# Chunked gated delta rule inside a two-layer block: token-major output of a chunk pair, its per-token norm on ScalarE, and a rewritten order of the mixer

## What is computed

```
proj = rms_norm(x) @ w_in            # attention q, k, v; delta q, k, v; gate z; beta, decay
attn = dilated_attention(q, k, v)    # 8 heads of 64
q = q * rsqrt(sum(q*q) + EPS) * K**-0.5;  k = k * rsqrt(sum(k*k) + EPS)     # 4 delta heads of 128
T = inverse(I + strict_lower(k_beta k^T * decay))       # per chunk of 64 tokens
scan over 8 chunks:
    v_new = u_i - w_i @ state
    o     = q_i @ state + (q_i k_i^T * decay) @ v_new
    state = state * gl + k_i^T @ v_new
dn_out = rms_norm(o, dn_norm_w) * silu(z)               # norm over the 128 values of a head, per token
x = x + rms_norm(concat(attn, dn_out) @ w_out)          # then a gated FFN
```

## Time and profile before

| | us |
|---|---|
| median of 3 runs | 3020.96 (3014.07 to 3027.36) |
| profiled execution | 3016.94 |
| its span in the trace | 3015.1 |
| PE busy | 2863.4 (95%) |
| DVE, ACT, POOL busy | 1192.5, 1126.0, 1225.2 (37 to 41%) |
| mean granted clock of PE, of full speed | 0.96 |

### The profile page before, as it was taken

The page is one execution under the profiler, slowest core; times in us unless marked ns, Lnnn a source line. Parts: engine busy times, 40 slices in busy tenths (PEclk is TensorE's granted clock), DMA queues, the critical chain, the costliest instruction groups (busy, mean ns, idle before and its releaser), DMA issues.

```text
span 3015.1 us, 44190 instructions
## 1 busy us (share of the span) xinstructions
PE 2863.4 (95%) x15452; PEld 2294.6 (76%) x15452; DVE 1192.5 (40%) x2248; ACT 1126.0 (37%) x1894; POOL 1225.2 (41%) x630
## 2 busy tenths in 40 slices
PE   9998999999999979999999988999999998899997
PEld 7777777888887767778888666778778666778776
DVE  3554426553065542455512576410013566410012
ACT  3453234443244622444433324532333324532331
POOL 2323033555433221355544452255553452255553
PEclk7998989999999989999999999999999998999998
DMA  3211012223322100122232211122222111122222
GB/s 117 73 47 43 2 49 71 96 95 100 104 68 74 44 29 13 52 84 96 92 105 91 66 63 50 36 83 98 91 98 84 59 65 48 37 83 98 91 97 91
DMA packets 62876, 217.29 MB, mean 72 GB/s; under 512 B 6576, under 2 KB 6704, under 8 KB 62480
## 3 DMA queue, kind: packets, MB, share of 16 engines
q1 hardware_dynamic: 62416, 214.28, 21.6%
q0 software_dynamic: 320, 1.12, 0.2%
HBM read 213.28 MB, written 2.10 MB: 71 GB/s over the span
## 4 chain that ended last, share of the span: by engine, by line
PE 79%; DVE 7%; ACT 4%; POOL 4%; issue 3%; DVEq 1%; ACTq 0%; DMA 0%; POOLq 0%; SPq 0%
PE bank L1784 51%; POOL wL L700 3%; PE bank L2102 3%; PE bank L1833 2%; PE bank L1961 2%; PE bank L1811 2%; PE bank L1962 2%; PE bank L1963 2%; PE bank L2013 2%; ACT wH L873 2%; PE bank L2002 1%; PE bank L1990 1%; PE bank L1841 1%; PE bank L1900 1%; PE bank L1848 1%
## 5 line engine op out<-in xcount | busy, mean ns | idle before, releaser
L700 POOL TENSOR_TENSOR wL<-raw,wH 128x1024 fp32r<-128x1024 f32 x380 | 922.4, 2428 | 1305.3 <-ACT wH L873 1305.3
L1784 PE MATMUL bank<-hH,wH 128*128 128x512 f32 x1744 | 722.3, 414 | 34.3 <-DVE pu L1341 17.5
L1784 PE MATMUL bank<-hL,wH 128*128 128x512 f32 x1744 | 685.6, 393 | 0.0
L1784 PE MATMUL bank<-hH,wL 128*128 128x512 f32 x1744 | 684.8, 393 | 0.0
L873 ACT ACTIVATE wH<-raw 128x1024 fp32r<-128x1024 f32 x380 | 399.5, 1051 | 264.9 <-PE bank L1784 236.0
L1784 PEld LDWEIGHTS bank<-hH,wH 128*128 128x128 f32 x1744 | 331.0, 190 | 155.9 <-issue 56.6
L1784 PEld LDWEIGHTS bank<-hH,wL 128*128 128x128 f32 x1744 | 331.2, 190 | 70.6 <-issue 10.3
L1784 PEld LDWEIGHTS bank<-hL,wH 128*128 128x128 f32 x1744 | 330.1, 189 | 71.6
L1784 PE MATMUL bank<-hidH,wH 128*128 128x512 f32 x864 | 338.0, 391 | 2.3 <-POOL wL L700 2.3
L1784 PE MATMUL bank<-hidH,wL 128*128 128x512 f32 x864 | 336.5, 390 | 0.0
L1784 PE MATMUL bank<-hidL,wH 128*128 128x512 f32 x864 | 336.5, 389 | 0.0
(11 more groups left out here) (325 smaller groups left out, 3969.7 us busy)
## 6 DMA issues: line engine op xcount, KB each, us to landing
raw<-w_dram SPq DMA_DIRECT2D x398, 512.0 KB, 3.4
x<-x_dram SPq DMA_DIRECT2D x4, 512.0 KB, 9.8
out_dram<-x SPq DMA_DIRECT2D x1, 2048.0 KB, 6.2
const<-const_dram SPq DMA_DIRECT2D x1, 1229.0 KB, 13.3
par_next<-par_dram POOLq DMA_DIRECT2D x5, 168.0 KB, 2.6
qkT<-pos_dram POOLq DMA_DIRECT2D x1, 256.0 KB, 7.1
const<-const_dram SPq DMA_DIRECT2D x1, 131.0 KB, 2.2
```

The lines of the kernel that those rows point to most:

```text
L700: pool.tensor_tensor(wL[:, s, :], raw[:, s, :], wH[:, s, :].bitcast(F32), ALU.subtract).then_inc(w_lo.sem, 1)
L1784: mm = pe.matmul((out or ACC[bk])[:, :], wt[:, s, c:c + P], rhs, start=first and k == 0 and j == 0, stop=last and k == tiles - 1 and j == 2)
```

## The change

The output of the scan becomes token-major and is made once per 128-token tile, after the second chunk (`delta_out` on PE): 64 tokens of q are stationary, the state moves, and the two chunks of the tile write partitions 0 to 63 and 64 to 127 of bank 7. So the norm of a token runs along the free axis: ACT squares the bank with an accumulated sum per head, and takes ln and exp(-0.5 x) of the four sums; DVE scales the bank into `dq` (`out_scale`), PE transposes it back (`delta_tile`), DVE multiplies by norm weight and silu(z) (`out_gate`), and the piece of the tile (128 tokens of all heads, no longer one head) is split at once. The token sums, the root and the spreading after the scan go. The state lives in three buffers in turn instead of two. In `ORDER`, `small` comes before `l2`, `l2` is split into k and q with `norm` entries of their own, the four attention pieces move from one place ahead of step 4 to one each behind steps 5, 8, 11 and 14, the SiLU of the gate moves there with them (two of the table loads with it), and all 32 first half-steps are in the table. At the start of the program PE runs 36 warm-up matmuls instead of 30.

```diff
 def mixer_order():
+    scans = []
+    for t in range(NT):
+        c = 2 * t
+        ahead = [("tile", t - 1, 0), ("gated", t - 1, 0)] if t % 2 else []
+        scans.append([("scan", c, 0), ("scan", c, 1)] + ahead + [("scan", c + 1, 0)]
+                     + [("scan", c + 1, 1)] * (t < NT - 1) + [("out", t, 0)])
+    scans = [scans[0] + scans[1][0:1] + [("scaled", 0, 0)] + scans[1][1:],
+             scans[2] + scans[3][0:1] + [("scaled", 2, 0)] + scans[3][1:]]
...
-    out += z[1] + [("pre", 0, 0)] + z[2][0:4] + [("pre", 0, 1)] + z[2][4:] + [("pre", 0, 2)] + z[3][0:4]
-    out += [("pre", 0, 3)] + z[3][4:] + [("pieces", 0, 0)]
-    out += [("pre", 0, k) for k in range(4, PRE)]
+    out += z[1][0:4] + [("pre", 0, 0), ("norm", 1, 0)] + z[1][4:] + [("l2", 0, 0)]
+    out += z[2][0:4] + [("pre", 0, 1)] + z[2][4:] + [("pre", 0, 2), ("norm", 0, 0)] + z[3][0:4]
+    out += [("pre", 0, 3)] + z[3][4:]
+    for k in range(4, PRE):
+        out += [("pre", 0, k)] + [("piece", f, 0) for f in range(4) if PIECE_AT[f] == k]
     for k in range(PRE):
-        out += [("pre", 1, k)] + scans[0][k - 1:k] * (1 <= k <= 12)
+        out += [("pre", 1, k)] + scans[0][k - 1:k] * (k >= 1)
+        out += [("scaled", 1, 0)] * (k == 15) + [("tile", 1, 0)] * (k == 16) + [("gated", 1, 0)] * (k == 18)
...
+    out += fill(HALVES_IN + 6) + [("scaled", 3, 0)]
+    done = HALVES_IN + 6
+    out += fill(done + 1) + [("tile", 3, 0), ("gated", 3, 0)]
...
         def state_of(c):
 
-            return sq[:, 0, :].rearrange("p (h c) -> p h c", c=P) if c % 2 else state[:, :, :]
+            return sq[:, c % 3 - 1, :].rearrange("p (h c) -> p h c", c=P) if c % 3 else state[:, :, :]
...
@block.scalar
+                    elif kind == "piece":
+                        if a == 0:
+                            act.wait_ge(unit_done.sem, unit_done.at(w, 28))
+                            use_table(SILU)
+                        piece_high(w, N_ATT1 + a, att_piece(0, a), att_place(w, a, hH), heads)
+                        act.wait_ge(acc_free[a % 2].sem, acc_free[a % 2].at(w, 13 + a // 2))
+                        act.activation(zT[:, a, :], zT[:, a, :], ACT.Silu).then_inc(z_ready.sem, 1)
+                        if a == HN - 1:
+                            use_table("natural_log_exp_and_others")
...
+                    elif kind == "out":
+                        act.wait_ge(out_done.sem, out_done.at(w, a + 1))
                         for h in range(HN):
+                            act.activation(kdec[:, a, h, :], OUT[:, h * P:h * P + P], ACT.Square,
+                                           accum_out=out_stat(a, 0)[:, h:h + 1])
+                        act.drain()
+                        act.activation(out_stat(a, 1), out_stat(a, 0), ACT.Ln, bias=cst("eps"), scale=1.0 / P)
+                        act.drain()
+                        act.activation(out_stat(a, 1), out_stat(a, 1), ACT.Exp, scale=-0.5).then_inc(out_rstd.sem, 1)
...
@block.vector
+            def out_scale(w, t):
+                dve.wait_ge(out_rstd.sem, out_rstd.at(w, t + 1))
+                dve.tensor_tensor(out_tile(t), heads(OUT[:, :]), per_head(out_stat(t, 1)),
+                                  ALU.mult).then_inc(out_scaled.sem, 1)
...
+            def out_gate(w, t):
...
+                dve.scalar_tensor_tensor(heads(piece[:, t % 2, :]), heads(DB[e % 3][:, :]), prm(w, "dnorm", 0, 1),
+                                         zT[:, :, t * P:t * P + P], ALU.mult, ALU.mult).then_inc(piece_ready.sem, 1)
...
@block.tensor
-            for _ in range(30):
+            for _ in range(36):
...
+            def delta_out(w, t):
+                pe.wait_ge(d_free[new % 3].sem, d_free[new % 3].at(w, new // 3 + 1))
+                pe.wait_ge(qdec_ready.sem, qdec_ready.at(w, t + 1))
...
+                for h in range(HN):
+                    for p0 in (0, CH):
+                        cc = slice(t * P + p0, t * P + p0 + CH)
+                        pe.matmul(OUT[p0:p0 + CH, h * P:h * P + P], dq[:, h, cc],
+                                  state_of(2 * t + p0 // CH)[:, h, :], start=True, stop=False)
+                    for p0 in (0, CH):
+                        mm = pe.matmul(OUT[p0:p0 + CH, h * P:h * P + P], qkT[p0:p0 + CH, t, h, 0:CH],
+                                       vn[p0:p0 + CH, h, :], start=False, stop=True)
+                mm.then_inc(out_done.sem, 1)
...
+            def delta_tile(w, t):
...
+                pe.wait_ge(out_scaled.sem, out_scaled.at(w, t + 1))
+                for h in range(HN):
+                    tr = pe.transpose(out[:, h * P:h * P + P], out_tile(t)[:, h, :], ident)
+                tr.then_inc(d_done.sem, 1)
...
-                for h in range(HN):
-                    pe.wait_ge(sq_ready.sem, sq_ready.at(w, 16 + h + 1))
-                    token_sums(lambda t, h=h: TRO[:, 4 * t + h:4 * t + h + 1], sq[:, h % 2, :], start=True,
-                               stop=True).then_inc(sq_used.sem, 1)
...
-                for h in range(HN):
-                    for t in range(NT):
-                        mm = pe.matmul(DSTAT[h][:, t * P:t * P + P],
-                                       root[:, 1, 4 * t + h:4 * t + h + 1].broadcast_to([P, P]), ident,
-                                       start=True, stop=True)
-                    mm.then_inc(dn_rstd.sem, 1)
```

More of the change, by code:

```diff
@@ L114, in mixer_order @@
         upto = HALVES_IN * (m + 1) // len(scans[1])
-        for i in range(done, upto):
-            out.append(("half", i // 4, i % 4))
-            if i % 4 == 1 and i > 4:
-                out.append(("hout", i // 4 - 1, 0))
+        out += fill(upto)
         done = upto
-    return out + [("hout", HALVES_IN // 4 - 1, 0)]
+    out += fill(HALVES_IN + 6) + [("scaled", 3, 0)]
+    done = HALVES_IN + 6
+    out += fill(done + 1) + [("tile", 3, 0), ("gated", 3, 0)]
+    done += 1
+    out += fill(4 * KD)
+    return out + [("hout", KD - 1, 0)]
 ORDER = mixer_order()
@@ L775, in _ @@
                         low_of(w, 26 + a)
-                    if kind == "pieces":
-                        for f in range(4):
-                            piece_low(w, N_ATT1 + f, att_piece(0, f), att_place(w, f, hL), att_place(w, f, hH), heads)
+                    if kind == "piece":
+                        piece_low(w, N_ATT1 + a, att_piece(0, a), att_place(w, a, hL), att_place(w, a, hH), heads)
+                    if kind == "gated":
+                        piece_low(w, N_DN1 + a, piece[:, a % 2, :], out_place(a, hL), out_place(a, hH), heads)
                     if kind == "hout":
@@ L1585, in _ @@
                         unit_scaled(w, 24 + a, zT[:, a, :], acc_free[a % 2].sem, SC)
[L1586 to L1589 removed]
+                    elif kind == "norm":
+                        for h in range(HN):
+                            normalise(w, a, h)
                     elif kind == "small":
```

156 lines of the change are left out of this document (68 added, 88 removed).

## The result

The changed kernel takes **2942.86 us** (median of 4 runs, 2939.82 to 2944.44) against 3024.16 us for the one before on the same chip (4 runs, 3014.07 to 3034.34): ratio 0.9751, 95% interval 0.9709 to 0.9793. Its profiled execution took 2941.83 us with a span of 2940.0; that of before had 3016.94 and 3015.1, so the spans differ by 75.1 us.

The account below looks back on a forecast made before the run. PE, with 79% of the chain, was taken to bound the kernel through its work, idle time or clock. Terms of -27.3 us per layer, -55 for two, and -9.5 at the start took 3016.9 to 2952 us, range 2929 to 2983.

Parts of the forecast that it names:

- First level: Wait for the first level mask: PE goes on at 272.05 instead of 277.04 as the pieces come later; -5.0 us per layer.
- Gate phase: PE's waits for DVE and the decays fall from 3.4 us to 1 with q and k split; -2.4 us per layer.
- Output of the scan: Four output steps of 3.3 us plus transposes of 3.7 replace eight steps totalling 23.2 us; -6.3 us per layer.
- New waits: In the scan, PE waits more around step 4 of pair 1 and behind ACT's norm chain; +4.4 us per layer, between 2 and 7.
- Tail: After the scan, 11.3 us of token sums, spreading and waits go; waits of 0.6, 0.6 and 0.5 come; -9.6 us per layer.
- Clock: In the mixer, part of the 19 us per layer lost to the low clock comes back; -8.4 us, between 0 and -14.
- Start: First norm, once: six more warm-up matmuls fill PE's 1.57 us gap; -9.5 us if the clock holds, otherwise 0.
- The start stays cold: Rival for the program start: closing the 1.6 us gap does not raise the clock; 2962 us, chance 0.27.
- Rival 4: Scan falls to the low clock from step 4 of pair 1 and stays there; slower, 3035 us, chance 0.04.

Follow-up runs that it names:

- Run 3: Changed kernel with the four attention pieces and the gate's SiLUs in one place again, ahead of step 4: 2947.11 us, ratio 0.9773.
- run 1: Kernel before with 36 warm-up matmuls instead of 30, nothing else: 3011.41 us, ratio 1.0009.
- run 4: Changed kernel with the norms of q and k together in the gate phase and `small` behind them, near the old order: 2943.19 us, ratio 0.9774.
- run 2: Changed kernel with 30 warm-up matmuls instead of 36, nothing else: 2940.29 us, ratio 0.9762.
- run 8: Changed kernel with five first-half steps moved from the second pair's scan into the waits of pair 1: 2931.25 us, ratio 0.9727.
- run 9: Changed kernel with twelve unused small matmuls ahead of the first level of the inverses, where PE waits for POOL: 2934.56 us, ratio 0.9769.
- run 12: Changed kernel with output products sorted by form, the second tile's output step later and nine half steps moved into waits: 2908.28 us, ratio 0.9675.

## Why the prediction was right, and where it was not

The time was forecast at 2952 in a range of 2929 to 2983, with 0.94 on faster; 2942.9 came. Per layer, in the prediction's own steps (measured per layer: the mean of the two, -30.3; waits and steps are read in layer 1):

- **First level, -5.0.** It measured -4.9, from the earlier trace rows and the waits above. Run 3 shows the mechanism, and that only some 3 us of it reach the end.
- **Gate phase, -2.4: the size came, the way failed.** The waits went from 3.4 to 3.9 us; I had said 1. k's products still wait 1.67 us for DVE and q's 1.94. The stage is shorter by 7.1 us, 4.9 of them the pieces; the other 2.2 are found in what releases the last gate weight on ACT. Before, and after:

```profile
267.86 1.06 ACT L873 ACTIVATE wH<-raw 128x1024 fp32r<-128x1024 f32 x1 [7.02 <-PE bank L1977]
```

```profile
253.15 1.06 ACT L912 ACTIVATE wH<-raw 128x1024 fp32r<-128x1024 f32 x1 [9.19 <-PE bank L2012]
```

PE's last matmul of the third gate projection releases ACT, behind it POOL makes the low part and the mask, and PE waits for the mask; so what delays PE ahead of this point does reach the end of the stage. The point lies 36.8 us behind the first gate step before (37.0 in layer 2, 36.9 in both layers of run 1), and 34.5 to 34.7 in the changed kernel and in every run on it, runs 3 and 4 included. Before, PE idled 3.5 us up to there and ran 6.8 us at the low level behind its wait of 2.7; in the changed kernel it idles 3.9 us with no low stretch, or (layer 2) 2.3 us with one of 3.4. So the 2.2 us are mostly clock, not waits. Which edit shortens the low stretch isn't shown; run 4, whose order comes near the old one, doesn't bring the 6.8 us back.
- **Output of the scan, -6.3.** Four steps at 3.70, 2.85, 2.94 and 2.94 us make 12.4, and transposes of 0.58, 0.56, 0.35 and 0.35 make 1.8: 14.3 against 23.2, **-8.9**. (In layer 2 the first step ran at the low level throughout and took 4.8 us.) The group of 0.36 us was read rightly from the earlier trace rows; the 0.05 us that I added to it for the second half of the array don't exist. The transposes were mis-sized by two: I took the row of eight (0.93 us) for one tile, and a tile has four.
- **New waits, +4.4.** They measured +1.8 at step 4, 0.5 ahead of the transposes and 1.39 behind tile 1's output: **+3.7**. ACT's chain took 1.8 us where I had 3.1, just below my bounds: the 0.40 us of the earlier trace rows was a square of another source, and the accumulator read overlaps the next square.
- **Tail, -9.6.** 11.3 us of bare work and waits went, one wait of 0.7 came: -10.6.
- **Clock, -8.4.** What is left of -30.3 is **-10**. As 28 us less at the low level are worth at most 14, this is in its bounds. It came from the gate phase and the second pair with its tail; beside pair 1 the clock did not rise (0.90, 0.87), where the first output step ran at the low level behind two waits for `xtb`.
- **Pair 1 as a whole** won nothing, as the steps say: old steps -11.6, new steps with one cold +6.6, transposes +1.1, waits +3.7.
- **Start, -9.5: the step that failed.** The profile shows -12.5, but run 1 shows that six more matmuls win nothing in the time (ratio 1.0009, and 2895.3 against 2894.6 us of work and 116.9 against 112.5 of clock in the table), and run 2 that the start can be at full clock without them. "The start stays cold" was no true rival either: in run 1 the start was at full clock and a long stretch at the low level stood in another norm. The right term was 0, with 10 us and more of spread in each execution.

Sum: the mixers gave 60.6 us where 55 were forecast, and 2 us came from the rest. Without the start term the forecast would have been 2962, 20 us above the profiled execution; 12.5 of these are the start that ran at full clock there. That 2952 lies nearer is partly luck: a term that the change doesn't earn made up for mixers forecast 6 us too small. In the terms of the table the forecast had 38 us of work and waits and 26 of clock, and 33 and 34 came. What makes a norm run at the low level, and whether the changed kernel meets it less often, stays open.

Rival 4, the scan at the low clock throughout, did not come. By the rule cited with it (TensorE: Matmul & The Clock Gate, Part 4 (PE-mode transpose), in the Trainium skill) the added transposes should not have helped the clock. The granted clock is 1.00 from 310 to 320 us, around those at 314.25, and from 342 to 382.8, around those at 360.88, so here four of them between other work did no harm.

## What to carry to other kernels

Count the changes of array form in a group of small matmuls, not the instructions: chunks side by side halved the step, and sorting by form took another 0.85 us of 2.9. Look at PE's waits together with the granted clock behind them: filling 3.2 us of waits with useful steps from elsewhere gave 7.4 us; a filler of no use in one gap left the mixers as they were. When a stage ends with a wait, follow the chain behind it to the engine that started it: here POOL's mask led back to PE's own gate projection. A clock gain seen at one place of one profile must be tried by that edit alone, on both kernels, before it is booked. Span times granted clock tells work from clock without a profile, and it varied by 13 us where the times of the kernel before varied by 45.

## What the chip showed that I had not expected

- A norm stage of unbroken matmuls ran for 24 to 31 us at the low level (0.50 to 0.54) in three profiles (from 14 us in the kernel before, from 2316 in run 1, from 789 in run 8), and at full clock in others, with the same instructions. It costs about half of that, 12 us and more.
- The times of the kernel before differ by up to 50 us (2984 to 3034) between executions, and where the granted clock is on record it accounts for nearly all of the difference: 0.971 in the one that took 2984.18 us, 0.958 in the one that took 3024.34, which is 86 and 127 us missing. Whether it is norms that make the difference isn't shown, as only one execution was profiled.
- A block of four instructions of one form, followed by one of the other form, takes 0.365 us like a block of two.
- Where low stretches lie differs between executions of equal mixers: from 275 to 285 us the clock was 0.83 in the changed kernel and 0.63 in run 2. A filled gap kept the stretch behind it at 1.00 in both layers (run 9) and left the mixer's time as it was; with the waits filled at three places (run 8) and five (run 12), mixers spent 10 to 14 us and 3 us at the low level, in place of 20.
